# Which engine subtracts the low part of U, block by block, and where the mixing loop keeps its starting states

## The reference, cut to what matters

```python
# token mixers: two chunked scans with states, chunk = 128 tokens
y_inter = einsum('bcihn,bchpn->bcihp', qc * exp(cum)[..., None], starts)   # starts: state ahead of each chunk
out = concatenate([y_ssd, y_ret], -1) @ w_out                              # 1024 x 1024
x = x + g1 * out
# peer: every token picks 8 x 16 of 16384 experts
act = gelu(einsum('tkd,td->tk', u_tab[ix], hx))
y = einsum('tk,tkd->td', gx * act, v_tab[ix])
```

## Time and profile before

| what | value |
|---|---|
| median of 3 runs | 3614.45 us (3613.23 to 3616.29) |
| profiled execution, its own time | 3615.19 us |
| its span, first to last instruction | 3613.5 us |
| mean granted TensorE clock | 0.966 of 2.4 GHz |
| mixing loop | about 675 to 915 us |
| U stage, plain blocks 0 to 59 | 1180 to 1725 us |
| U stage, gate-building blocks 60 to 123 | 1733 to about 2495 us |
| U stage, blocks 124 to 127 | to 2529 us |
| outputs stage | 2532 to 3609 us |

### The profile page before, as it was taken

The page is one execution under the profiler, slowest core; times in us unless marked ns, Lnnn a source line. Parts: engine busy times, 40 slices in busy tenths (PEclk is TensorE's granted clock), DMA queues, the critical chain, the costliest instruction groups (busy, mean ns, idle before and its releaser), DMA issues. The chain is left out here.

```text
span 3613.5 us, 50302 instructions
## 1 busy us (share of the span) xinstructions
PE 3330.6 (92%) x17854; PEld 2994.0 (83%) x17854; DVE 2813.8 (78%) x4693; ACT 1252.5 (35%) x2299; POOL 1653.7 (46%) x1014
## 2 busy tenths in 40 slices
PE   5989969599799999899999999999799999999997
PEld 2989959554799999899899999999688888888886
DVE  3555237497477799999787888886699999999998
ACT  2331135233322221222666666665222222222221
POOL 0000012111111477776777777776365556555550
PEclk8999979799899999999999999999899999999999
DMA  4235334452111477776788888888999999999994
GB/s 170 101 129 174 109 105 146 161 147 88 53 36 36 148 246 251 239 248 213 273 315 316 320 321 322 317 317 299 321 365 366 360 375 365 367 360 369 371 363 161
DMA packets 379005, 880.27 MB, mean 244 GB/s; under 512 B 32530, under 2 KB 198946, under 8 KB 375682
## 3 DMA queue, kind: packets, MB, share of 16 engines
q1 hardware_dynamic: 256004, 390.58, 33.0%
q0 software_dynamic: 115600, 423.31, 31.9%
q10 hardware_dynamic: 7280, 65.01, 4.7%
HBM read 740.61 MB, written 138.18 MB: 243 GB/s over the span
## 5 line engine op out<-in xcount | busy, mean ns | idle before, releaser
L1842 POOL DMA_INDIRECT hT<-peer_v,hT x372 | 547.2, 1471 | 444.7 <-DVE hrow L1863 329.4
L1702 PE MATMUL ps<-h_hi,u_hi 128*128 128x384 f32 x2048 | 701.7, 343 | 37.5 <-POOL u_lo L1591 29.8
L1702 PE MATMUL ps<-h_lo,u_hi 128*128 128x384 f32 x2048 | 691.1, 337 | 0.0
L1702 PE MATMUL ps<-h_hi,u_lo 128*128 128x384 f32 x2048 | 690.5, 337 | 0.0
L1965 PE MATMUL ps<-v_hi,a_hi 128*128 128x512 f32 x1536 | 598.7, 390 | 22.9 <-DVE ga_rest L1880 20.4
L1965 PE MATMUL ps<-v_hi,ga_rest 128*128 128x512 f32 x1536 | 598.3, 389 | 0.0
L1965 PE MATMUL ps<-vw_rest,a_hi 128*128 128x512 f32 x1536 | 598.3, 389 | 0.0
L1863 DVE SCALAR_TENSOR_TENSOR hrow<-hT,dots,hrow 128x1024 f32<-128x1024 f32 x372 | 457.3, 1285 | 0.0
L1591 POOL TENSOR_TENSOR u_lo<-uw,u_hi 128x1024 fp32r<-128x1024 f32 x126 | 334.0, 2651 | 202.4 <-ACT u_hi L1499 201.2
L1702 PEld LDWEIGHTS ps<-h_hi,u_hi 128*128 128x128 f32 x2048 | 390.7, 191 | 41.5 <-issue 38.7
L1587 POOL DMA_INDIRECT hT<-u_rows,hT x212 | 342.6, 1616 | 120.5 <-DVE dots L1612 71.0
(11 more groups left out here) (327 smaller groups left out, 5660.4 us busy)
## 6 DMA issues: line engine op xcount, KB each, us to landing
uw<-u_T SPq DMA_DIRECT2D x128, 512.0 KB, 4.2
vw<-peer_v SPq DMA_DIRECT2D x128, 512.0 KB, 9.0
s_d<-so SPq DMA_DIRECT2D x256, 192.0 KB
gates_d<-big ACTq DMA_DIRECT2D x24, 2048.0 KB, 9.7
gt<-gates_d SPq DMA_DIRECT2D x32, 1536.0 KB, 28.6
ga<-s_d SPq DMA_DIRECT2D x128, 384.0 KB, 9.7
wmr<-w_modT SPq DMA_DIRECT2D x32, 512.0 KB, 4.1
tok_d<-st SPq DMA_DIRECT2D x54, 216.0 KB, 4.1
```

The costliest lines, as they stand in the source:

```text
L1702: mm = pe.matmul(g.ps[4 + 2 * s + b][:, 0:HALF], u[s][:, k, :], h[:, k, b * HALF:(b + 1) * HALF], start=(k == 0 and i == 0), stop=(k == KD ...
L1842: pool.indirect_dma_start(rows[n % NU], None, g.v_rows, bass.IndirectOffsetOnAxis(ap=g.pick[m % GT][:, m // GT:m // GT + 1], axis=0)).then ...
```

## The change

In the mixing loop: the latent states get buffers of their own (`sf_latent`, and `sr_latent` in the tile `gained`, which is free until then), loaded right behind the first chunk's tiles; chunk 1 reads from there; VectorE's `states(2)` waits for the store of the prompt's states. ScalarE waits for the first chunk's six tiles before it issues the load of wo.

```diff
+        sf_latent = sb("sflatent", [P, W_])
+        f_state = lambda n: sf_latent if n == 1 else sf[n % 2]
+        r_state = lambda n: sr_latent if n == 1 else sr[n % 2]
...
+        sr_latent = gained[0:HD].rearrange("p k (f d) -> p k f d", f=2)
...
                 sp.dma_start(xt[n % 2][:], g.x_all[n * P:(n + 1) * P, :]).then_inc(x_loaded[n % 2], 16)
             load(0)
+            sp.dma_start(sf_latent[:], g.ssd_fwd_T).then_inc(latent_in, 16)
+            sp.dma_start(sr_latent[:, :, 0, :], g.ret_fwd_T.rearrange("n (h d) -> n h d", h=HEADS)).then_inc(latent_in, 16)
...
                     sp.dma_start(g.ssd_f_out, sf[1][:]).then_inc(states_out, 16)
                     sp.dma_start(g.ret_f_out.rearrange("n (h d) -> n h d", h=HEADS), sr[1][:, :, 0, :]).then_inc(states_out, 16)
-                    sp.wait_ge(states_out, 32)
-                    sp.dma_start(sf[1][:], g.ssd_fwd_T).then_inc(states_out, 16)
-                    sp.dma_start(sr[1][:, :, 0, :], g.ret_fwd_T.rearrange("n (h d) -> n h d", h=HEADS)).then_inc(states_out, 16)
...
                     load_x(n + 1)
+            sp.wait_ge(states_out, 32)
...
-                pool.tensor_copy(sr[s][:, :, 1, :], h8(g.SBr[:, b, :])).then_inc(sr_copied, 1)
+                pool.tensor_copy(r_state(n)[:, :, 1, :], h8(g.SBr[:, b, :])).then_inc(sr_copied, 1)
...
+            act.wait_ge(loaded[0], 96)
             act.dma_start(wo[:], g.w_out.rearrange("(k p) n -> p k n", p=P)).then_inc(wo_in, 16)
...
                 dve.wait_ge(loaded[s], 96 * (n // 2 + 1))
                 if n == 1:
-                    dve.wait_ge(states_out, 64)
+                    dve.wait_ge(latent_in, 32)
+                if n == 2:
+                    dve.wait_ge(states_out, 32)
                 if n:
                     dve.wait_ge(inter_done, n)
-                dve.tensor_tensor(h8(scaled[:]), h8(sf[s][:]), row8(g.CD, n, 0), ALU.mult)
-                link(dve.tensor_tensor(h8(scaledr[0:HD, :]), sr[s][:, :, 0, :], heads_bcast(g.CD[0:HD, NT, 0:8]), ALU.mult))
+                dve.tensor_tensor(h8(scaled[:]), h8(f_state(n)[:]), row8(g.CD, n, 0), ALU.mult)
+                link(dve.tensor_tensor(h8(scaledr[0:HD, :]), r_state(n)[:, :, 0, :], heads_bcast(g.CD[0:HD, NT, 0:8]), ALU.mult))
...
                 if n == 0:
                     pe.wait_ge(zeroed, 1)
                 elif n == 1:
-                    pe.wait_ge(states_out, 64)
+                    pe.wait_ge(latent_in, 32)
...
-                    pe.matmul(g.ps[0][:, cols], c, sf[s][:, cols], start=True, stop=True)
+                    pe.matmul(g.ps[0][:, cols], c, f_state(n)[:, cols], start=True, stop=True)
...
                     mm = pe.matmul(g.ps[2 + h // 4][:, (h % 4) * P:(h % 4 + 1) * P], qT[s][:, h, :],
-                                   sr[s][:, h].rearrange("p f d -> p (f d)"), start=True, stop=True)
+                                   r_state(n)[:, h].rearrange("p f d -> p (f d)"), start=True, stop=True)
```

```diff
+        u_lo_mid = sem("ulomid")
...
-            def load(e, s):
-                sp.wait_ge(u_lo_ready, e - 1)
+            def load(e, s, freed, many):
+                sp.wait_ge(freed, many)
                 sp.dma_start(uw[s][:], g.u_T[bass.ds(e, 1)].rearrange("o p k c -> p (o k) c")).then_inc(u_loaded[s], 16)
-            load(2, 0)
-            load(3, 1)
-            with sp.Fori(0, NE // 2 - 2) as j:
-                for s in range(2):
-                    for b in range(2):
-                        store(j * 2 + s, b)
-                    load(j * 2 + (s + 4), s)
+            load(2, 0, u_lo_ready, 1)
+            load(3, 1, u_lo_ready, 2)
+            for j0, j1, freed, base in ((0, H1 // 2 - 1, u_lo_ready, 3), (H1 // 2 - 1, H2 // 2 - 1, u_lo_mid, 3 - H1),
+                                        (H2 // 2 - 1, NE // 2 - 2, u_lo_ready, 3 + H1 - H2)):
+                with sp.Fori(j0, j1) as j:
+                    for s in range(2):
+                        for b in range(2):
+                            store(j * 2 + s, b)
+                        load(j * 2 + (s + 4), s, freed, j * 2 + (s + base))
...
             for e in range(NE):
                 if e < H1:
-                    turn = slots_between(U1, 6, H1 - 4, e)
+                    turn = slots_between(U1, 6, H1 - 1, e)
...
                 for n in slots_between(V1, H2 - 1, NE - 2, e):
                     gather(GT * NSEL + n)
-                if e + 2 < NE:
+                if e + 2 < H1 or H2 <= e + 2 < NE:
...
+            def low(e):
+                dve.wait_ge(u_hi_ready, e + 1)
+                dve.tensor_tensor(u_lo[e % 2][:], uw[e % 2][:], f(u_hi[e % 2][:]), ALU.subtract).then_inc(u_lo_mid, 1)
...
+            low(H1)
             for p in range(PAIRS):
                 many = u_rows_by(H1 + 2 * p + 1) - u_rows_by(H1 + 2 * p - 1)
                 for i in range(THREE):
                     group(p * THREE + i)
+                    if i and (p or i == 2):
+                        low(H1 + 2 * p + i - 1)
                     n = dots(n, many * (i + 1) // THREE - many * i // THREE)
...
-            def half(e, s, b, first=False):
+            def half(e, s, b, first=False, split=u_lo_ready, base=0):
                 if b == 0:
-                    pe.wait_ge(u_lo_ready, e + 1)
+                    pe.wait_ge(split, e + (base + 1))
                 if not first:
                     pe.wait_ge(act_done, e * 2 + (b - 3))
                 for k in range(KD):
...
-            def hidden(e, s, first=False):
-                half(e, s, 0, first)
+            def hidden(e, s, first=False, base=0):
+                half(e, s, 0, first, u_lo_ready, base)
...
                             product(m * (2 * THREE) + (k // 2 * THREE + i), k // 2 * THREE + i)
-                        half(m * 4 + (H1 + k), k % 2, b)
+                        half(m * 4 + (H1 + k), k % 2, b, False, u_lo_mid, -H1)
             with pe.Fori(H2 // 2, NE // 2) as j:
-                hidden(j * 2, 0)
-                hidden(j * 2 + 1, 1)
+                hidden(j * 2, 0, False, H1 - H2)
+                hidden(j * 2 + 1, 1, False, H1 - H2)
```

More of the change, by code:

```diff
@@ L958, in mix_tokens @@
         g1, wo, gained = sb("g1", [P, D]), sb("wo", [P, KD, D]), sb("gained", [P, KD, P])
+        sr_latent = gained[0:HD].rearrange("p k (f d) -> p k f d", f=2)
         xn = gained[:].rearrange("p k c -> p (k c)")
-        gn_in, nw_in, wo_in, g1_in = sem("gnin"), sem("nwin"), sem("woin"), sem("g1in")
+        gn_in, nw_in, wo_in, g1_in, latent_in = sem("gnin"), sem("nwin"), sem("woin"), sem("g1in"), sem("latent")
         rs_ready, xn_ready, turned, tile_ready, last_root, last_ms = sem("rs"), sem("xn"), sem("turned"), sem("tile"), sem("lroot"), sem("lms")
```

## The result

| | before | changed |
|---|---|---|
| median of four runs | 3615.37 us (3613.23 to 3619.55) | 3549.66 us (3544.43 to 3556.83) |
| ratio to before | | 0.9816, 95% interval 0.9802 to 0.983 |
| profiled execution | 3615.19 us | 3544.43 us |
| its span | 3613.5 us | 3542.8 us |

The change saves 66 us, 1.8%; 55 were predicted. The direction was right and the range too short on the side of the gain.

A forecast was written before the change was run, and what follows sets the result against it. VectorE with its row waits was taken to bound the gate-building blocks. Gains of 44 + 1 + 10 = 55 us from 3615.19 gave 3560.2, stated as 3559.5 us for the median, with a range from 3549 to 3588.

The forecast's parts named there:

- the chain: Gate-building blocks: GpSimd's subtraction waits for ScalarE and holds up gathers; rows, VectorE, ScalarE and TensorE then run late.
- Gate-building blocks, 44 us: Moving the subtraction from GpSimd to VectorE brings pairs of blocks from 23.83 to 22.22 us: gain 44, between 29 and 50.
- 5 us of leftover row waits: Gate-building blocks: a guess of 5 us for VectorE's waits for gathered rows that would remain after the change.
- 11.9 + 1.5: Start of the gate-building blocks: 11.9 us for the part beyond 31 pairs, 1.5 for a first product at cold clock.
- upper bound of 50: Gate-building blocks: the most that moving the subtraction was expected to gain, 50 us.
- Contention: Gate-building blocks: GpSimd's subtractions lengthen VectorE's instructions, 1.6 us each; relieved, VectorE needs 18.4 us a pair, otherwise 21.7.
- Rival 1: Gate-building blocks: row waits come from DMA and stay; gain 29 us in place of 44, total 3575; chance 0.21.
- rival 2: Gate-building blocks: VectorE was full and gets 78 us more; pairs take 26.2 us, total 3680; chance 0.09.
- rival 3: Gate-building blocks: TensorE waits at ScalarE or the stores of s_d, most of the 44 us is lost; 3604; chance 0.07.
- point of decision: Gate-building blocks: rival 2 decides as soon as a pair's demand on VectorE passes 23.83 us.
- Seam, 1 us: Plain blocks' end: wider-spread gathers save at most 2.5 us, the subtraction ahead costs 1.2; gain 1, between -2 and 3.
- Mixing loop, 10 us: First load 6.9 us earlier, latent-state wait of 4.6 gone, 1.5 off for late wo; gain 10, between 3 and 13.

The follow-up runs named there:

- U1 = 80: The changed kernel with 80 in place of 128 dots in the plain blocks, the rest moved into the gate-building blocks: 3513.71 us, ratio 0.9719.
- U1 = 96: The changed kernel with 96 in place of 128 dots in the plain blocks, 32 moved into the gate-building blocks: 3523.88 us, ratio 0.9748.

## Why the prediction was right or wrong

- **What bounds the kernel, and the chain.** Right. VectorE with its row waits was the full engine: the pairs of the kernels here follow max(22.0, VectorE's busy time + its row waits), from 19.3 + 4.5 before to 18.5 + 2.6 with GpSimd's wait put back and 23.3 with three subtractions. Where rows are late the sum only says that VectorE has no other idle time; why they are late must be read from GpSimd, whose queue was held in the kernel before and was full in the one with 9 rows and GpSimd subtracting.
- **Gate-building blocks, 44 us: the term that was mis-sized; it measured 51.6.** The step that failed is "without waits a pair takes 1912.75 - 2.09 - 1888.44 = 22.22 us". It takes 22.00. The wait of 2.09 is counted from the end of the matmul before, but matmuls are pipelined: without a wait a product starts 0.16 us ahead of the last one's recorded end (in the changed kernel, 1741.41 is such a start, and the matmul of 1741.23 ahead of it is recorded to 1741.56). The delay was 2.09 + 0.16, and the product at 1888.44 was 0.03 us longer than the usual 1.95; the last 0.03 of the 0.22 is left open. The trace of the kernel before could have told it, one pair earlier:

```profile
1866.33 2.05 PE L1717 MATMUL ps<-hT 128*128 128x128 f32 x16 [1.56 <-ACT hT L1551]
```

  From this third product to the one at 1888.44 TensorE waited for nothing, and it is 22.11 us, 0.10 of it in a first product of 2.05 in place of 1.95. 0.22 x 31 is 6.8 us. The 5 us of leftover row waits didn't come; against them stands a slower start: the first two products took 3.78 and 3.39 us with a wait of 2.26 between, and the third came after 18.1 us (1713.24 to 1731.30) where 11.9 + 1.5 had been set down, 4.7 us more. Together that is 6.8 + 5 - 4.7 = 7.1 us, against 51.6 - 44.4 = 7.2 missed. The upper bound of 50 carried the same error and so was no bound.
- **Why the rows were late.** Right (late issue, not DMA): the longer lead shows it. That the subtraction had to move for it was taken for granted and is wrong: the lead alone does it.
- **Contention.** Right that it was there and that 18.4 us would be needed (18.5). Its price was too small, 1.6 us for each subtraction where 2.2 holds with a busy VectorE. It had no part in the result as long as rows come in time: a VectorE at 20.5 us is as good as one at 18.5. The rule that I drew on, from the Trainium skill ("SBUF — State Buffer", who interferes with whom), agrees with the kernel with the extra subtraction, where each of 59 GpSimd subtractions lengthened VectorE's instructions by 2.17 to 2.22 us.
- **Rival 1** (row waits stay, 0.21), **rival 2** (VectorE overfull, 0.09) and **rival 3** (waits at ScalarE or the stores, 0.07) all fell. ScalarE waited 49.6 us for the stores of s_d, and TensorE stayed busy throughout. Rival 2's mechanism is real, and its point of decision was well placed: the kernels with three subtractions and with an extra one on GpSimd pass it.
- **Seam, 1 us:** measured 3.1. VectorE's end was the bound, as said, but it came 2.1 us earlier itself (540.4 us after the stage's start, 542.5 before), and it does so because of the spread (542.7 without). TensorE's transposes then start 0.1 us behind it, where they were 2.5 us late. Against that stand the subtraction, 1.14, and slower transposes after 19.44 us of idling (3.61 us in place of 3.00). That the spread "hardly pays", 2.5 us at most, was too low: its one profile says 5.
- **Mixing loop, 10 us:** measured 13.0 in the profile, and 13 in the total of the kernel with this part alone, whose own profile says 9.6; the difference between the two profiles goes with the clock. The first load gained 8.4 us, not 6.9 (8.5 us alone, where the later load of the same tiles took 10.05), and the 1.5 us for a late wo wasn't needed: it landed after 22.1 us, at 701.3, ahead of 704.93.
- **The range** was built from bounds of terms that were themselves too low (50 where 51.6 came); it missed by 1.1 us, which is within the noise. Of the profiled difference of 70.7 us, 51.6 + 3.1 + 13.0 = 67.7 belong to these three terms and 5.2 to unchanged code ahead of the mixing loop, which I take for chance; 2.2 us were lost again elsewhere, most of it (1.5) between the first product with wo and the U stage.

## What to carry to other kernels

When an engine that works in order both computes and issues gathers, first ask how far ahead the gathers are issued: here a lead of 11 rows in place of 8 was worth as much as moving 64 instructions to another engine. A longer lead makes rows timely but leaves the engine as full as it was, so its sum must be made too: 21.1 us of 22.0 with 8 rows left no room for a ninth. A relief only counts up to the next bound, so a part of a change can be worth nothing until the slack that it makes is filled: moving the subtraction gave 0 us with 8 rows a pair and 36 with 9, and filling the slack (U1 = 80) gave another 36. And a period of a pipelined engine is to be measured from start to start between waits, not by subtracting a wait that is counted from a modelled end.

## What the runs showed of the hardware that was not expected

- A GpSimd subtraction of 128x1024 costs a full VectorE queue 2.2 us, most of its own 2.56. Beside indirect gathers VectorE's dots keep their 1.22 us, but the gathers take 1.97 us in place of the 0.95 that they take beside an idle VectorE.
- DMA at a share of 0.98 (373 GB/s, U1 = 96 from 1710 to 2380) still took half a row more per pair, with pairs at 22.00 us: 363 GB/s in the outputs stage and 387 GB/s with U1 = 80 both read as 1.00. The same share can thus stand for different throughputs, and 1.00 at 363 GB/s doesn't show that no more would pass.
- Unchanged code ahead of the mixing loop varies by up to 5.9 us between executions (its start at 670.1 to 676.0). With two runs each, effects of 5 us were seen in the profile only.
